# The gate/up bias of a mixture of experts: added in the accumulation of every block, or kept in a bank of its own per visit of an expert

## What is computed

```python
def expert_block(args):
    e, tok, wt = args
    xb = xt[tok]
    gu = xb @ w_gate_up[e] + b_gate_up[e]
    gate = jnp.minimum(gu[:, :D_EXPERT], SWIGLU_LIMIT)
    up = jnp.clip(gu[:, D_EXPERT:], -SWIGLU_LIMIT, SWIGLU_LIMIT)
    act = (up + 1.0) * gate * jax.nn.sigmoid(SWIGLU_ALPHA * gate)
    yb = act @ w_down[e] + b_down[e]
    return yb * wt.astype(yb.dtype)[:, None]
```

## Time and profile before

| | us |
|---|---|
| median of three runs (1304.44 to 1307.55) | 1305.67 |
| the profiled execution | 1307.32 |
| its span, from the first to the last instruction | 1305.6 |
| TensorE, matmuls busy | 1259.9 |
| VectorE / ScalarE / GpSimd busy | 521.2 / 189.9 / 162.6 |

### The profile page before, as it was taken

The page is one execution under the profiler, slowest core; times in us unless marked ns, Lnnn a source line. Parts: engine busy times, 40 slices in busy tenths (PEclk is TensorE's granted clock), DMA queues, the critical chain, the costliest instruction groups (busy, mean ns, idle before and its releaser), DMA issues.

```text
span 1305.6 us, 52682 instructions
## 1 busy us (share of the span) xinstructions
PE 1259.9 (97%) x21821; PEld 747.6 (57%) x21821; DVE 521.2 (40%) x1733; ACT 189.9 (15%) x437; POOL 162.6 (12%) x267
## 2 busy tenths in 40 slices
PE   7999999999999999999999999999999999988885
PEld 4446654545666665665665665666656656644552
DVE  6454223447333333343343343333433433422337
ACT  3431123332001000000000000010000000000002
POOL 4100330122101101101011011011011010000111
PEclk9999999999999999999999999999999999999998
DMA  6453131619999999999999999999999999999997
GB/s 224 147 193 131 34 130 49 258 65 342 404 421 407 421 410 422 417 420 410 419 416 421 412 422 414 422 417 420 413 416 421 416 421 417 420 421 421 421 425 283
DMA packets 80504, 455.73 MB, mean 349 GB/s; under 512 B 11057, under 2 KB 23018, under 8 KB 30730
## 3 DMA queue, kind: packets, MB, share of 16 engines
q1 hardware_dynamic: 76400, 445.69, 83.8%
q0 software_dynamic: 3888, 8.40, 1.7%
q10 hardware_dynamic: 106, 0.04, 0.0%
HBM read 432.53 MB, written 23.27 MB: 349 GB/s over the span
## 4 chain that ended last, share of the span: by engine, by line
PE 52%; DMA 44%; DVE 2%; issue 1%; SPq 0%; ACT 0%; POOL 0%; POOLq 0%; ACTq 0%; DVEq 0%
DMA ring<-in_w_gate_up_dram 26%; PE ps L1924 18%; DMA ring<-in_w_down_dram 16%; PE ps L1492 11%; PE ps L1976 8%; PE ps L1512 4%; PE ps L1890 3%; PE ps L1553 2%; DMA x_rows_dram<-cat,rowi 1%; PE ps L1916 1%; PE ps L1546 1%; PE ps L1967 0%; DMA ring<-in_x_dram 0%; DMA ring<-x_rows_dram 0%; PE ps L1899 0%
## 5 line engine op out<-in xcount | busy, mean ns | idle before, releaser
L1924 PE MATMUL ps<-ring,cat 128*32 128x256 f32 x9856 | 550.1, 380 | 7.6 <-DMA ring<-in_w_gate_up_dram 7.6
L1924 PEld LDWEIGHTS ps<-ring,cat 128*32 128x32 f32 x9856 | 306.6, 110 | 219.9 <-DMA ring<-in_w_gate_up_dram 10.9
L1976 PE MATMUL ps<-ring,cat 128*32 128x256 f32 x4800 | 276.2, 380 | 13.2 <-DMA ring<-in_w_down_dram 12.6
L1976 PEld LDWEIGHTS ps<-ring,cat 128*32 128x32 f32 x4800 | 142.6, 110 | 118.1 <-DMA ring<-in_w_down_dram 11.3
L1492 PE MATMUL ps<-hbuf,ring 128*128 128x512 f32 x320 | 147.7, 608 | 1.7 <-DVE hbuf L922 1.7
L1313 DVE TENSOR_REDUCE wslot<-ps 128x2 f32<-128x6 f32 x75 | 12.4, 165 | 318.7 <-ACT cat L848 317.1
L606 POOL DMA_INDIRECT pair_rows_dram<-cat,rowi x73 | 72.7, 996 | 432.1 <-ACT cat L848 432.1
L840 ACT ACTIVATE cat<-cat 128x128 f32<-128x128 f32 x154 | 47.7, 309 | 516.8 <-DVE cat L1337 516.8
L1890 PE MATMUL ps<-hbuf,cat 128*32 128x256 bf16 x2432 | 105.2, 273 | 0.6 <-DVE cat L1410 0.6
L1492 PEld LDWEIGHTS ps<-hbuf,ring 128*128 128x128 f32 x320 | 58.9, 192 | 68.2 <-issue 65.8
L1337 DVE TENSOR_SCALAR cat<-ps 128x128 f32<-128x128 f32 x154 | 44.8, 291 | 128.8 <-PE ps L1924 128.7
(11 more groups left out here) (369 smaller groups left out, 818.5 us busy)
## 6 DMA issues: line engine op xcount, KB each, us to landing
ring<-in_w_gate_up_dram SPq DMA_DIRECT2D x256, 1024.0 KB, 10.0
ring<-in_w_down_dram SPq DMA_DIRECT2D x128, 1024.0 KB, 9.9
ring<-in_w_in_dram SPq DMA_DIRECT2D x10, 1024.0 KB, 6.3
pair_rows_dram<-cat SPq DMA_DIRECT2D x4, 2048.0 KB, 10.9
ring<-pair_rows_dram SPq DMA_DIRECT2D x4, 2048.0 KB, 20.6
ring<-in_w_out_dram SPq DMA_DIRECT2D x1, 4096.0 KB, 12.9
ring<-in_x_dram SPq DMA_DIRECT2D x4, 512.0 KB, 5.4
x_rows_dram<-ring SPq DMA_DIRECT2D x2, 1024.0 KB, 9.7
```

Of the source, the lines that this page charges most:

```text
L1924: last = mm(ps[SLOTS * q:SLOTS * (q + 1), banks[half], 0:2 * P].rearrange("p (s m r) -> p s m r", s=2, m=2), x[:, SLOTS * u:SLOTS * (u + 1 ...
L1976: last = mm(ps[SLOTS * q:SLOTS * (q + 1), 1, 0:QD], actT[:, c // 4, SLOTS * (c % 4):SLOTS * (c % 4 + 1)], w[:, i, q * QD:(q + 1) * QD], st ...
```

## The change

For the experts from 1 on, TensorE makes the bias product once per visit, in front of its loop (`expert_bias`), into bank 6, both halves side by side. In each block, the first unit of the gate/up product now opens banks 4 and 5 (`opens=True`), and the last matmul of the first half of the first unit tells `gub_used`. ScalarE copies each half of bank 6 into one of two buffers (`biased`) in each block, ahead of that half's sigmoid. VectorE adds the copy to the sums in PSUM for gate and up and clamps the results in SBUF: four instructions instead of two. The two early blocks and expert 0's loop keep the bias in the accumulation. `biased` lies where `actT_first` and `ys_first` had their data, so the copy of half 1 waits for `late_out` (the late scatters), and `ident_late` moves to another place. `first_ok` gives its place to the semaphore `bias_copied`; its waiters wait for `ebc_ok` instead.

```diff
-        ident_late = cat[:, 1792:1920]
+        ident_late = aux[:, 2048:2048 + P]
+        biased = [cat[:, 2048:2304], cat[:, 1792:2048]]
...
+            def copy_bias(g, half):
+
+                act.wait_ge(gub_used, g + 1)
+                act.wait_ge(actt_ok, 2 * g)
+                if half:
+                    act.wait_ge(late_out, 2 * 16)
+                A(biased[half], ps[:, BIAS, 2 * P * half:2 * P * (half + 1)], ACT.Copy).then_inc(bias_copied, 1)
...
+            def activate(g, first):
+
+                if first:
+                    A(sm[:, 12:13], epsc[:, 0:1], ACT.Copy).then_inc(bias_copied, 2)
+                    sigmoids(g)
+                else:
+                    for half in range(2):
+                        copy_bias(g, half)
+                        sigmoid_half(g, half)
...
+                if bias is None:
+                    V.tensor_scalar(chunked_half(gc[:, half]), in_order(ps[:, b, 0:P]), LIMIT, None, ALU.min).then_inc(gc_ok, 1)
...
+                else:
+                    dve.wait_ge(bias_copied, 2 * g + (half + 1))
+                    V.tensor_tensor(chunked_half(gc[:, half]), in_order(ps[:, b, 0:P]), in_order(bias[half][:, 0:P]),
+                                    ALU.add).then_inc(uc_step, 1)
+                    V.tensor_tensor(chunked_half(uc[:, half]), in_order(ps[:, b, P:2 * P]), in_order(bias[half][:, P:2 * P]),
+                                    ALU.add).then_inc(uc_step, 1)
+                    dve.wait_ge(uc_step, n * 4 + 1)
+                    V.tensor_scalar(gc[:, half], gc[:, half], LIMIT, None, ALU.min).then_inc(gc_ok, 1)
+                    dve.wait_ge(uc_step, n * 4 + 2)
+                    V.tensor_scalar(uc[:, half], uc[:, half], -LIMIT, LIMIT, ALU.max, ALU.min).then_inc(uc_step, 1)
...
+            def expert_bias(begin):
+
+                pe.wait_ge(sel_step, 2 * begin)
+                pe.wait_ge(actt_ok, 2 * begin)
+                bias_rows_of(lambda half: ps[:, BIAS, 2 * P * half:2 * P * (half + 1)], True, True)
...
+                if opened is not None and u == 0 and half == 0:
+                    last.then_inc(opened, 1)
...
             def expert_block(g, e):
 
-                gate_up_bias(g, (gu_bank(0), gu_bank(1)))
-                gate_up(e, (gu_bank(0), gu_bank(1)))
+                if e == 0:
+                    gate_up_bias(g, (gu_bank(0), gu_bank(1)))
+                    gate_up(e, (gu_bank(0), gu_bank(1)))
+                else:
+                    ready(g)
+                    gate_up(e, (gu_bank(0), gu_bank(1)), opens=True, opened=gub_used)
...
                 begin, upto = upto, pe.value_load(tab[0:1, e + 1:e + 2], min_val=2, max_val=MAXB)
+                expert_bias(begin)
                 with pe.Fori(begin, upto) as g:
                     expert_block(g, e)
```

More of the change, by code:

```diff
@@ L235, in gu_bank @@
             return (4, 5)[half]
+        BIAS = 6
         def late_bank(i):
@@ L295, in moe_block @@
             "fin_sum", "fin_sq", "fin_rt", "fin_o", "stored", "act_step")]
[L296 to L297 removed]
+        bias_out, bias_home, gi_ok, less_ok, h2p_ok, bias_copied = [sem(n) for n in (
+            "bias_out", "bias_home", "gi_ok", "less_ok", "h2p_ok", "bias_copied")]
         late_out = sem("late_out")
@@ L848, in activate @@
                 A(ys, ps[:, 1, 0:QD], ACT.Copy, scale=wslot[:, 0:1]).then_inc(ys_ok, 1)
+            A(sm[:, 12:13], epsc[:, 0:1], ACT.Copy).then_inc(bias_copied, 4)
             for g in range(2):
@@ L1328, in slots_of_first, with swiglu_half @@
                 V.tensor_copy(sm[:, 38 + i:39 + i], wslot_first[i][:, 0:1]).then_inc(slot_ok, 1)
-            def swiglu_half(g, half, done, b, to=actT, told=actt_ok, by=1):
+            def swiglu_half(g, half, done, b, to=actT, told=actt_ok, by=1, bias=None):
                 n = 2 * g + half
@@ L1412, in _, with swiglu @@
             blocks = dve.value_load(tab[0:1, E:E + 1], min_val=E, max_val=MAXB)
-            def swiglu(g):
+            def swiglu(g, bias):
                 slots_of(g)
@@ L1422, in swiglu @@
                 for half in range(2):
-                    swiglu_half(g, half, g * NU + NGU, gu_bank(half))
+                    swiglu_half(g, half, g * NU + NGU, gu_bank(half), bias=bias)
                 rows_T(g + 2)
-            dve.wait_ge(first_ok, 1)
+            dve.wait_ge(ebc_ok, 1)
             first = dve.value_load(first_n[0:1, 0:1], min_val=FIRST, max_val=MAXB)
             with dve.Fori(2, first) as g:
-                swiglu(g)
+                swiglu(g, None)
             dve.wait_ge(side_ps, 1)
             with dve.Fori(first, blocks) as g:
-                swiglu(g)
+                swiglu(g, biased)
             for b in range(TB - 1):
@@ L1906, in landed, with bias_rows_of, ready @@
                 return ring[:, slot * UNIT:(slot + 1) * UNIT].rearrange("p (s c) -> p s c", s=2)
-            def gate_up_bias(g, banks, start=True):
+            def bias_rows_of(to, start, stop):
                 bias = bias3[:, 0:2 * D].rearrange("p (s c) -> p s c", s=2)
+                for half in range(2):
+                    for q in range(Q):
+                        last = mm(to(half)[SLOTS * q:SLOTS * (q + 1)].rearrange("p (s m r) -> p s m r", s=2, m=2),
+                                  selu[:, :], quarter(bias, q, half), start=start, stop=stop)
+                return last
+            def ready(g):
                 pe.wait_ge(xgt_ok, g + 1)
@@ L1913, in gate_up_bias, with gate_up_unit @@
                     pe.wait_ge(actt_ok, 2 * g)
-                for half in range(2):
-                    for q in range(Q):
-                        last = mm(ps[SLOTS * q:SLOTS * (q + 1), banks[half], 0:2 * P].rearrange(
-                            "p (s m r) -> p s m r", s=2, m=2), selu[:, :], quarter(bias, q, half), start=start, stop=False)
-                last.then_inc(gub_used, 1)
-            def gate_up_unit(e, u, half, banks, x, skip, opens):
+            def gate_up_bias(g, banks, start=True):
+                ready(g)
+                bias_rows_of(lambda half: ps[:, banks[half], 0:2 * P], start, False).then_inc(gub_used, 1)
+            def expert_bias(begin):
+                pe.wait_ge(sel_step, 2 * begin)
+                pe.wait_ge(actt_ok, 2 * begin)
+                bias_rows_of(lambda half: ps[:, BIAS, 2 * P * half:2 * P * (half + 1)], True, True)
+            def gate_up_unit(e, u, half, banks, x, skip, opens, opened):
                 w = landed(e, u)
```

33 lines of the change are left out of this document (16 added, 17 removed).

## The result

The changed kernel takes 1308.22 us in the median of 22 runs (1305.18 to 1311.28); the kernel before, beside it, 1304.82 us (1303.14 to 1307.55). The ratio is 1.0022, 95% interval 1.0015 to 1.0029: **slower**, by 2.0 to 3.8 us. The forecast was no change, 1305.2 us, and its range ended at 1307.8, so it was wrong in sign and size. The profiled execution, 1305.44 us with a span of 1303.6, is the second shortest of the 22.

A forecast was written before the change was run, and what follows sets the result against it. The prediction took the weight stream, almost balanced with TensorE, to end the loops. -2.0 us from TensorE and +1.5 for the new wait gave -0.5 us on the profiled execution, 1305.2 us against the median; range 1301.5 to 1307.8.

The forecast's parts named there:

- What bounds the kernel: Whole loops: weight stream and TensorE balanced almost exactly, TensorE holding 380 us of the chain, weights the last 300 us.
- Rival 1: Loops: TensorE is the bound after all, gain 5.1 us, 1300.6 us; chance 0.20.
- What goes from TensorE: Blocks inside visits: 43 bias products of 0.22 us go, 9.5 us less on TensorE.
- My 2.0: Gain taken to reach the end time: half of the at most 4.0 us where TensorE holds the chain.
- Visits, VectorE and ScalarE: Visit starts add 0.05 us each, 1.6 us on TensorE; longer VectorE chains and ScalarE's copies in each block cost nothing.
- Rivals 2 and 3: Slower: visit starts at 0.45 us each, 1311.6 us, chance 0.09; VectorE's chain late in each block, chance 0.03.
- rival 4: Visits: the bias product isn't really saved, because each visit has one block; no chance given.
- A new wait at one place: Expert 1's first block: half 1's copy waits for the second late scatter, costing the stream 1.5 us, 0.8 to 2.1.
- The sum: Whole kernel: -2.0 from TensorE and +1.5 from the wait give -0.5 us, no change that can be told.

The follow-up runs named there:

- kernel without the wait: The changed kernel with the copied bias put into free halves of `act_` and `actT`, so no copy waits for the late scatter: 1305.32 us, ratio 0.9998.
- TensorE's part alone: The changed kernel without copies, adds and wait, gate/up bias left out from expert 1 on; bias product still once per visit: 1304.5 us, ratio 0.9996.
- pair of kernels with the product twice: Bias product put back in each block beside the visit's: in the changed kernel 1315.32 us, ratio 1.0074; in the kernel without the wait 1311.69 us, 1.0043.
- the run with 20 matmuls: The changed kernel with expert 1's first block peeled off and 20 extra matmuls, results unused, ahead of its wait for half 1: 1307.36 us, ratio 1.0015.
- the second execution of the change: Profiled execution from a rerun of the unaltered changed kernel: span 1309.7 us; the rerun took 1310.93 us, ratio 1.004 to the kernel before.

## Why the prediction was wrong

- **What bounds the kernel: right.** The weights do. Taking 9.5 us from TensorE gave 0.5 us (interval -0.7 to 1.8). Rival 1, TensorE as the bound with 1300.6 us, is out. The Trainium skill's ceiling of 435 GB/s (DMA: Bandwidth & Descriptors, Bandwidth), by which the stream would have had room, is not what the stream keeps up in any run here; 418 to 422 is its rate in the late stretch.
- **What goes from TensorE: right in size, too high in what arrives.** Blocks of 12.08 to 12.12 us and 272 matmuls are there. I took half of 4.0 us as arriving because the chain changes sides four times; the medians say 0.3 to 0.5 (kernel without the wait, TensorE's part alone). My 2.0 lies just outside what the interval of TensorE's part alone allows (1.8). Single profiles say more, 1.4 to 1.8 us without the wait and 3.1 to 3.5 for TensorE's part alone, and can't settle it. By the medians this term was some 1.5 us too high, the smaller part of the miss: with it put right and the wait at 1.5 us, the sum would be +1.0 to +1.2 us, the right sign, inside the range and still no change that can be told.
- **Visits, VectorE and ScalarE: right.** From the visit's product to its first gate/up matmul it is 0.24 us on the mean of 25 visits from 400 to 1155 us in the first profile, where a block of the kernel before had 0.22, so a visit adds 0.02 us there (I had taken 0.05). That the rest costs nothing is shown by the kernel without the wait, which has all of them and stands at 0.9998. Rivals 2 and 3 are out, and the 272 matmuls exclude rival 4.
- **The step that failed is "A new wait at one place".** Place, chain and victim were right: scatter, copy of half 1, down product, block 4's first unit, the stream. The size, 1.5 us with bounds 0.8 and 2.1, was wrong. The runs show 3.5 to 4.0 us (with and without the wait in one batch, by ratios and by medians), 4.0 again by the pair of kernels with the product twice, and 2.5 with the wait put into the kernel before. The 1.5 us is what the executions with an early landing and a held clock lose, and it was luck that the first profile was one. (By the prediction's own figures the wait is 353.9 - 351.9 = 2.0 us and not 2.1, and its 358.7 adds 1.9 to 356.79; neither matters here.)
- Two assumptions made it so small. First, "lands 5.9 us later at the earliest": I took the lower end of the earlier trace rows, though the row itself reached 6.7, and in three of six profiles of the change the second scatter took 7.5 to 7.8 us. TensorE's wait is 3.5 to 4.0 us there instead of 2.2 to 2.3. Second, I priced the matmuls behind the wait at full clock, and the clock fell in four of six profiles. No row that I had taken out showed such a fall, but the trace of the kernel before has it, in the late stretch where TensorE waits for weights. TensorE by time, there:

```profile
1203.40 1.07 PE L1976 MATMUL ps<-ring,cat 128*32 128x256 f32 x16 [2.48 <-DMA ring<-in_w_down_dram]
1205.82 1.83 PE L1976 MATMUL ps<-ring,cat 128*32 128x256 f32 x16 [1.35 <-DMA ring<-in_w_down_dram]
```

The same 16 matmuls take 1.83 us instead of 1.07, and the granted clock from 1205 to 1210 us is 0.66; at 13.71 us, behind 1.66 us of idling, the clock had fallen too (shown above). So the rival could have been written down with a price from this trace.
- **The sum, made again** with the runs' sizes: -0.3 for all that the change does without the wait, +3.5 for the wait (1.0025 less 0.9998, of 1305) is +3.2 us. Measured are 2.9 by the ratio and 3.4 between the medians. This agrees almost by construction, since the 3.5 comes from runs of the change itself; with the 2.5 us of the wait put in alone it is +2.2. The range should have reached up to a wait that costs 3.5 to 4 us, and "this wait costs more than it lasts" was missing among the rivals; it was the one on the slower side that decided.
- **Left open:** why the same scatter lands 1.4 to 1.7 us later in some executions, and how much of the wait's 3.5 to 4.0 us is the clock. Single profiles show 1.5 to 2.8 us for it where it falls; in the medians the only sign is the run with 20 matmuls, where the interval overlaps that of the change. The price of the wait as a whole is shown, its split into late landing and fallen clock is not.

No version here beats the kernel before. The change without its wait equals it, since the product that it saves is hidden behind the weights.

## What to carry to other kernels

Where two resources are balanced, as here, work taken from one can buy almost nothing while work added costs most of itself, so an edit that saves on one of them must not touch the other. A buffer that a late DMA still reads is worth more than its bytes: look for a home that is free by the program's own order (here, the halves that the same chain writes last) before accepting a wait "once". And a wait on the path is priced by its worst landing and by what the waiting engine does afterwards, not by the shortest row of one profile.

## What the runs showed of the hardware

- TensorE's granted clock can fall behind a single idle stretch in a program that is otherwise dense, and how long TensorE idled does not alone decide it. In block 3, behind 3.5 to 4.0 us of idling it fell in three of three profiles (means of 0.66 to 0.83 from 350 to 360 us) and behind 7.3 us in another (0.66 from 355 to 365); behind 2.15 to 2.33 us it held twice and fell once (0.83); behind 1.59 to 1.85 us it held in four of four. At 13.7 us, behind 1.66 us of idling, it fell in both profiles of the kernel before and held in all six of the change. In block 3, 32 matmuls took 2.67 to 3.64 us behind a fall instead of 1.93. Matmuls whose results nobody reads kept it at 1.00 in the wait, in three of three profiles.
- One indirect scatter of the same shape, near the same place, took 5.9 to 7.8 us from issue to landing in 18 profiles. It took over 7 us also in the run with TensorE's part alone (7.25), where no block waits for it.
- The first load behind a gap in the stream landed about 4.8 us behind its issue (361.37 to 366.22 us in the second execution of the change), as the prediction's estimate of 4.9 had it.
